# The causal mask of the next chunk moved from GpSimd to VectorE in a chunked SSD and mLSTM mixer

## What is computed

```python
causal = jnp.tril(jnp.ones((q, q), dtype=bool))
seg = acs[:, :, :, None] - acs[:, :, None]
decay = jnp.exp(jnp.where(causal[:, :, None, None], seg, -jnp.inf))
y_diag = jnp.einsum('bclsg,bclsgj,bcsgjp->bclgjp', cb, decay, xdt)
```

## Time and profile before

| what | value |
|---|---|
| median of 3 runs | 3790.77 us (3787.42 to 3794.9) |
| the profiled execution's own time | 3788.31 us |
| its span, first to last instruction | 3786.3 us |
| granted TensorE clock, mean | 0.916 |
| busy: PE, DVE, ACT, POOL | 83%, 39%, 26%, 9% |
| the mixers | about 1561 to 1985 us of the span |
| the add of the mask on GpSimd | x16, one for each chunk |

### The profile page before, as it was taken

How to read it: one execution, slowest core, us unless ns; L and a number is a source line. 1 busy time by engine, 2 the same in 40 slices (tenths; PEclk the granted TensorE clock), 3 DMA queues, 4 the chain that set the end, 5 groups by cost and what they waited for, 6 DMA issues and landing times. The chain is left out here.

```text
span 3786.3 us, 38003 instructions
## 1 busy us (share of the span) xinstructions
PE 3151.9 (83%) x14848; PEld 2603.4 (69%) x14848; DVE 1463.6 (39%) x1756; ACT 969.9 (26%) x1580; POOL 329.4 (9%) x307
## 2 busy tenths in 40 slices
PE   3899889999932264488887986999999999999998
PEld 2677777999931132266665875888788878887886
DVE  5134343100047682488772332332433243323322
ACT  4222222111111021233332332232323222222222
POOL 0000000000000010244430110000000000000000
PEclk9999999999965576699998998999999999999999
DMA  2222222211100314656646753223323232323222
GB/s 89 73 69 86 94 89 77 89 67 62 47 21 7 38 35 131 205 196 233 236 162 254 269 221 133 100 92 120 133 100 116 99 131 100 123 106 117 100 100 78
DMA packets 151292, 435.57 MB, mean 115 GB/s; under 512 B 13910, under 2 KB 82422, under 8 KB 125174
## 3 DMA queue, kind: packets, MB, share of 16 engines
q1 hardware_dynamic: 112694, 301.56, 23.3%
q0 software_dynamic: 25024, 98.58, 7.5%
q10 hardware_dynamic: 13440, 33.56, 2.6%
HBM read 313.47 MB, written 120.18 MB: 115 GB/s over the span
## 5 line engine op out<-in xcount | busy, mean ns | idle before, releaser
L1892 PE MATMUL f_banks<-f_h_hi,f_w_hi 128*128 128x512 f32 x1408 | 552.0, 392 | 48.1 <-DVE f_w_lo L1842 48.1
L1892 PE MATMUL f_banks<-f_h_lo,f_w_hi 128*128 128x512 f32 x1408 | 550.9, 391 | 0.0
L1892 PE MATMUL f_banks<-f_h_hi,f_w_lo 128*128 128x512 f32 x1408 | 550.7, 391 | 0.0
L1842 DVE TENSOR_TENSOR f_w_lo<-f_raw,f_w_hi 128x2048 fp32r<-128x2048 f32 x132 | 302.7, 2293 | 395.6 <-ACT f_w_hi L1774 395.5
L1892 PEld LDWEIGHTS f_banks<-f_h_hi,f_w_hi 128*128 128x128 f32 x1408 | 266.5, 189 | 105.4 <-DVE f_w_lo L1842 49.8
L1774 ACT ACTIVATE f_w_hi<-f_raw 128x2048 fp32r<-128x2048 f32 x132 | 251.4, 1905 | 284.2 <-PE f_banks L1903 275.3
L402 PE MATMUL c_banks<-h_hi,c_w_hi 128*128 128x512 f32 x672 | 271.4, 404 | 45.3 <-DVE c_w_lo L343 45.3
L1892 PEld LDWEIGHTS f_banks<-f_h_lo,f_w_hi 128*128 128x128 f32 x1408 | 266.5, 189 | 55.5
L1892 PEld LDWEIGHTS f_banks<-f_h_hi,f_w_lo 128*128 128x128 f32 x1408 | 266.2, 189 | 55.6
L1903 PE MATMUL f_banks<-f_w_hi,f_a_hi 128*128 128x512 f32 x704 | 273.9, 389 | 0.0
L1903 PE MATMUL f_banks<-f_w_hi,f_a_lo 128*128 128x512 f32 x704 | 273.9, 389 | 0.0
(11 more groups left out here) (340 smaller groups left out, 4739.9 us busy)
## 6 DMA issues: line engine op xcount, KB each, us to landing
f_raw<-in_w_gu SPq DMA_DIRECT2D x88, 1024.0 KB, 4.8
f_raw<-in_w_dn SPq DMA_DIRECT2D x44, 1024.0 KB, 4.8
tokmaj<-t_out POOLq DMA_DIRECT2D x48, 384.0 KB, 2.9
m_bc<-rows SPq DMA_DIRECT2D x16, 1152.0 KB, 7.0
conv<-c_conv POOLq DMA_DIRECT2D x16, 1024.0 KB, 4.1
o_y_hi<-y_hi SPq DMA_DIRECT2D x16, 1024.0 KB, 4.7
o_y_lo<-y_lo SPq DMA_DIRECT2D x16, 1024.0 KB, 7.3
tok<-c_tok POOLq DMA_DIRECT2D x24, 512.0 KB, 3.8
```

The source lines that it names most:

```text
L1842: tt(w_lo[:, u % 2], raw[:, s % 2], w_hi[:, u % 2].bitcast(F32), ALU.subtract).then_inc(wlo_ok, 1)
L1892: last = nc.tensor.matmul(banks[:, q % 2, 2 * (i % 2) + g, :], w[:, u % 2, at], h[:, k, :], start=k == 0 and j == 0, stop=k == KD - 1 and ...
```

## The change

VectorE adds the mask. Its add for chunk 0 stands before the loop, and the one for chunk c + 1 right behind L1348 of chunk c, in front of the second `lower_y`. It carries the wait for the five loads of chunk c + 1 with it. GpSimd keeps xde, xskip, the add to off, and ve; as xde and xskip read `tk`, GpSimd now waits for the loads of chunk c at the head of its chunk.

```diff
@@ gpsimd
-            def masked(c):
-                pool.wait_ge(in_[c % 2], (c // 2 + 1) * 16 * LOADS)
-                nc.gpsimd.tensor_tensor(bc[:, c % 2], bc[:, c % 2], mask[:].unsqueeze(1).to_broadcast([P, NBC, P]),
-                                        ALU.add).then_inc(mask_ok, 1)
-
-            masked(0)
             for c in range(TT):
                 b = c % 2
                 x = tk[:, b, X_C:X_C + XW].rearrange("p (h d) -> p h d", h=HS)
+                pool.wait_ge(in_[b], (c // 2 + 1) * 16 * LOADS)
                 if c >= 1:
                     pool.wait_ge(state_mm, c)
...
                 nc.gpsimd.tensor_tensor(ve[:], va[:, b], over(col(c, 2, FR, HM), DA), ALU.mult).then_inc(ve_ok, 1)
-                if c + 1 < TT:
-                    masked(c + 1)
@@ vector
+            def masked(c):
+                dve.wait_ge(in_[c % 2], (c // 2 + 1) * 16 * LOADS)
+                tt(bc[:, c % 2], bc[:, c % 2], mask[:].unsqueeze(1).to_broadcast([P, NBC, P]), add).then_inc(mask_ok, 1)
...
             dve.wait_ge(set_ok, 1)
+            masked(0)
             for c in range(TT + 1):
...
                 tt(y[:, b, 0:XW], y[:, b, 0:XW], zo[:, b, 0:XW], mul).then_inc(gated_ok, 1)
+                if c + 1 < TT:
+                    masked(c + 1)
                 if c >= 1:
                     lower_y(c - 1, 1)
```

## The result

The changed kernel takes 3810.33 us (median of 5 runs, 3807.39 to 3814.4), the kernel before beside it 3794.9 us (3787.42 to 3795.72). The ratio is 1.0046, with a 95% interval of 1.0031 to 1.0061: slower by 15 us on the medians and by some 17 us on the ratio. A second set of runs of the same kernel gave 1.0042 (1.0028 to 1.0055). The forecast was 12.5 us slower, 3803 us.

What follows compares the result with a forecast made beforehand. No engine was full; a chain of waits tied the chunks. After the change a load loop of 26.3 us binds: 13 loops cost 13.1 us more, the last chunk gains 0.6; 3790.8 + 12.5 = 3803 us, range 3783 to 3822.

Steps and rivals of the forecast that it cites:

- What bounds: In the mixers before the change: no engine full, chunks tied by waits, GpSimd's mask off the chain in late chunks.
- Part 1, the mask on VectorE: The mask takes 2.58 us per chunk in series on VectorE, between 2.29 and 5.1 us.
- Part 2, what comes back: VectorE freed from GpSimd's mask: L1348 4.9 to 0.96 us in four chunks, L1295 6.53 to 2.35, L1366 gains 0.6.
- Part 3, the wait: VectorE's wait for five loads closes a loop through the next bc load: 26.3 us per chunk, 24.6 to 27.7.
- the tail: From lower_y behind the mask to num: 4.26 us, the middle between 3.46 and 5.06.
- The sum: Over the mixers: 13 loops of 26.3 us, 341.9 against 328.8, less 0.6 in the last chunk: +12.5 us.
- Rival A2, the port: GpSimd's xde goes first and the mask waits 1.47 us: loop 27.8 us, +32 us, 3823 us; chance 0.13.
- Rival B, VectorE's own chain: VectorE's serial work binds instead of the loads: 24.6 us per chunk, -7.2 us, about 3784 us; chance 0.20.
- Rival C, faster: TensorE's clock holds at L1439 and loads land sooner: 24.0 us per chunk, -15 us, 3776 us; chance 0.10.

Runs made afterwards that it cites:

- e5: The kernel before, mask still on GpSimd, but that mask waits for the load of bc alone: 3765.0 us, ratio 0.9928.
- e10: e5 plus 8 filler matmuls on TensorE ahead of its wait for L1322 in chunks 3 to 15: 3745.6 us, ratio 0.9873.
- e1: The changed kernel, but VectorE's mask waits for the load of bc alone instead of all five loads: 3756.5 us, ratio 0.9901.
- e3: The changed kernel, with the mask and its wait for five loads moved behind L1348's followers to ahead of L1363 and num: 3784.4 us, ratio 0.9975.
- e4: The changed kernel, with 14 filler matmuls on TensorE ahead of the third transposes in chunks 3 to 14: 3789.3 us, ratio 0.9989.
- e0: The changed kernel run once more, unaltered: 3809.6 us, ratio 1.0042.
- e7: e1 with two output projection pieces on TensorE moved from ahead of L1448 to ahead of the third transposes: 3755.3 us, ratio 0.9902.
- e8: e7 with the add of xskip to off moved from GpSimd to VectorE: 3764.4 us, ratio 0.9928.
- e2: The kernel before, mask on GpSimd, with only the wait for the next chunk's five loads added on VectorE behind L1348: 3783.4 us, ratio 0.9971.

## Why the prediction was right, and where it was off

- **What bounds.** Right. The mask was off the chain in the late chunks; e5 and e10 keep GpSimd's 5.8 us and are faster.
- **Part 1, the mask on VectorE.** Forecast 2.58 us, measured 2.56.
- **Part 2, what comes back.** y times gate fell from 4.4 and 4.9 to 1.2 us (forecast 0.96) and L1366 to 0.17. L1371 and L1372 also gave back 12.3 us in all, which the forecast left out; they stand behind the mean. The gain up to the `bc` load of chunk 3, forecast 4.0 us, was 4.8, counted from the first load of the phase to that load (72.8 us before, 68.0 after). The two w_lo pieces of chunk 0 fell from 6.53 to 3.08 us, not to 2.35.
- **Part 3, the wait.** The mechanism was right: e1 takes the loads out of the loop and e3 takes the loop off the mask, and both fall below the kernel before. Load issued to mask started was forecast at 19.5 us, and the loads of chunks 4 to 15 took 18.6 to 20.3, 19.55 in the mean. (Of the nine pairs behind the forecast the shortest is chunk 5's, 18.81 us, not 18.87.) The term that was mis-sized is the tail. I took 4.26 us, the middle between a full and a partly lowered clock; it was 5.1 us in chunk 10 and 4.7 to 5.8 in the other chunks from 3 to 14, 5.2 in the mean. TensorE now idles some 3.9 us there each time, and e4, which fills that time, brings the tail back to 3.46 us. So the period was 27.3 us instead of 26.3. Over 13 loops that is 13 us; profile against profile the mixers cost 25 us more, the forecast 12.5.
- **The sum.** "328.8 us before (25.3 each)" was put badly: that figure runs from the issue after the change, 1619.7. Before, the 13 periods took 1948.5 - 1623.7 = 324.8 us, 25.0 each. The result of the sum is not touched.
- **On the medians** the loss was 15 to 17 us, less than the 26 us between the two profiled executions. The one before (3788.3) lies low among the 22 runs of that kernel beside e1 (3781.5 to 3798.6, median 3793.1), the one after (3814.4) is the slowest of its five. An estimate of where the difference lies: outside the mixers the twelve profiled executions took 3358 to 3366 us whatever the kernel, so a median run of the kernel before spends some 425 to 435 us in the mixers (first load to num of chunk 15), not the 421.4 of the profiled one; both profiles of the changed kernel show 446 to 447. The sum built on a short baseline and on a short tail, and the two errors took most of each other away. The mechanism was right; that the forecast loss came within 2 to 5 us of the measured one was in part luck.
- **Rival A2, the port.** It did not happen in the profile of the result: every mask took 2.55 or 2.56 us. In chunk 10 GpSimd's xde started at 1857.52, VectorE's mask at 1857.47, and xde took the delay:

```profile
1857.52 3.84 POOL L1270 TENSOR_TENSOR m_xde<-m_tk,tok_cols 128x768 f32<-128x768 f32 x1 [2.99 <-DMA m_zo<-tokmaj]
```

  3.84 us instead of 1.47, and its end, 1861.36, holds nobody up. Where both were released by the same landing, VectorE was ahead by 0.04 or 0.05 us in every chunk. Chunk 2 of e0 is the other order: xde was first and the mask took 3.82 us, in one chunk of 16. The Trainium skill ("SBUF — State Buffer", section "Who interferes with whom") says that issue order decides who blocks; this trace, chunk 2 of e0 and both cases of e5 agree.
- **Rival B, VectorE's own chain.** Not in the changed kernel. It binds in e1, at 23.2 us where I had worked out 24.6: the head runs at full clock there.
- **Rival C, faster.** Half of it took place: with the change the clock at the head was full, and the time from L1320 to y fell to 8.1 us. The loads hid the gain, as forecast. e1 shows it without them.

## What to carry to other kernels

When an operation moves to another engine, its wait moves too, and on an engine that runs in order everything written behind it then waits for things that it does not need. Give the moved operation the narrowest semaphore: here a wait for one load instead of five turned +0.46% into -1%. And look at what the next load waits for: if that stands behind the moved wait, a loop of load latency and work is closed, and its length is the new period.

## What the runs showed that was not expected

- Eight matmuls into an unused bank, 1.8 us of filler per chunk, made the kernel before 0.67% faster. TensorE had idled 2.1 to 2.9 us at the head of chunks 9 to 15, and the granted clock of the following 3.4 us was 0.51 to 0.65 in those read. In e1 it idled 1.5 us there, and the clock stayed at 1.00. The idle time alone does not settle it: in e5 the clock was once full and once low behind 2.7 us.
- The low clock costs twice: 1.3 us in the matmuls at the head, and, as y comes late, first place at the port to GpSimd, where y times gate took 4.9 instead of 1.2 us (e5).
- The profile put a wait of 1.46 us down to L1448 in most kernels with a full clock at the head; e7 and e8 show that in theirs it ended with GpSimd's add.
- The wait alone (e2) made the kernel about 0.3% faster. Why is left open.
